# Splitting the query and key tiles of the latent attention two heads ahead and taking its scores in three passes: a case on one core of Trainium2

## The reference, cut to what matters

```python
q = (_rms_norm(cq, q_norm) @ w_uq).reshape(b, s, H, MLA_NOPE + MLA_ROPE)       # 64 + 32 per head
...
kv = (_rms_norm(ckv, kv_norm) @ w_ukv).reshape(b, s, H, MLA_NOPE + MLA_V)
k_nope, v = kv[..., :MLA_NOPE], kv[..., MLA_NOPE:]
...
sc = (jnp.einsum('bqhd,bkhd->bhqk', qn, k_nope) + jnp.einsum('bqhr,bkr->bhqk', qr, k_rope)) * scale
p, _ = _probs(sc, k_pos[None, :] <= t[:, None])
return jnp.einsum('bhqk,bkhd->bqhd', p.astype(v.dtype), v)
```

## Time and profile before

| | |
|---|---|
| median of three runs | 3776.79 us (3770.28 to 3781.73) |
| time of the profiled execution | 3777.02 us |
| its span | 3775.1 us |
| PE busy | 3430.8 us, 91% of the span |
| DVE busy | 2023.8 us, 54% |
| ACT busy | 1225.2 us, 32% |
| granted TensorE clock, mean | 0.927 of full |

### The profile page before, as it was taken

The page is one execution under the profiler, slowest core; times in us unless marked ns, Lnnn a source line. Parts: engine busy times, 40 slices in busy tenths (PEclk is TensorE's granted clock), DMA queues, the critical chain, the costliest instruction groups (busy, mean ns, idle before and its releaser), DMA issues.

```text
span 3775.1 us, 46102 instructions
## 1 busy us (share of the span) xinstructions
PE 3430.8 (91%) x16505; PEld 2822.2 (75%) x16505; DVE 2023.8 (54%) x2745; ACT 1225.2 (32%) x1897; POOL 239.9 (6%) x206
## 2 busy tenths in 40 slices
PE   8999998999999999989999994498899966879999
PEld 6888776887888788865778882398688854867887
DVE  7753433647743675355465435676555356545553
ACT  3222321543222322233432222454333231533332
POOL 1000101001000100022010004300000011010000
PEclk9999995999989999988999996699899978999999
DMA  5532241014532353211045320265233221013332
GB/s 168 175 106 89 82 110 24 1 43 135 161 95 95 114 175 106 89 55 34 29 123 168 110 95 22 62 175 169 67 100 100 89 72 39 1 45 89 91 104 72
DMA packets 390900, 347.51 MB, mean 92 GB/s; under 512 B 11344, under 2 KB 343437, under 8 KB 390669
## 3 DMA queue, kind: packets, MB, share of 16 engines
q1 hardware_dynamic: 390797, 346.16, 30.7%
HBM read 344.02 MB, written 2.10 MB: 92 GB/s over the span
## 4 chain that ended last, share of the span: by engine, by line
PE 81%; DVE 10%; ACT 3%; issue 2%; POOL 2%; SPq 1%; DMA 0%; ACTq 0%; DVEq 0%; POOLq 0%
PE ps L802 24%; PE ps L803 23%; PE ps L804 23%; PE ps L890 4%; PE ps L879 2%; PE ps L1285 2%; POOL sq_sum L2229 2%; ACT w_hi L1338 1%; DVE w_lo L1351 1%; DVE rstd L1716 1%; PE ps L867 1%; DVE a_lo L1693 1%; DVE x_T L2213 1%; PE ps L998 1%; DVE sq_att L2009 1%
## 5 line engine op out<-in xcount | busy, mean ns | idle before, releaser
L802 PE MATMUL ps<-a_hi,w_hi 128*128 128x512 f32 (+1 forms) x2968 | 1144.5, 386 | 134.8 <-DVE a_lo L1977 43.8
L803 PE MATMUL ps<-a_lo,w_hi 128*128 128x512 f32 (+1 forms) x2968 | 1129.9, 381 | 0.0
L804 PE MATMUL ps<-a_hi,w_lo 128*128 128x512 f32 (+1 forms) x2968 | 1128.9, 380 | 0.0
L802 PEld LDWEIGHTS ps<-a_hi,w_hi 128*128 128x128 f32 x2968 | 570.1, 192 | 279.3 <-issue 115.2
L1351 DVE TENSOR_TENSOR w_lo<-w_raw,w_hi 128x1024 fp32r<-128x1024 f32 (+1 forms) x536 | 636.3, 1215 | 183.4 <-ACT w_hi L1338 168.8
L1338 ACT ACTIVATE w_hi<-w_raw 128x1024 fp32r<-128x1024 f32 (+1 forms) x536 | 549.6, 1044 | 308.0 <-PE ps L804 306.1
L804 PEld LDWEIGHTS ps<-a_hi,w_lo 128*128 128x128 f32 x2968 | 571.1, 192 | 104.0
L803 PEld LDWEIGHTS ps<-a_lo,w_hi 128*128 128x128 f32 x2968 | 572.2, 193 | 100.9 <-issue 1.0
L802 PE MATMUL ps<-hs_hi,w_hi 128*128 128x512 f32 (+1 forms) x1232 | 465.1, 378 | 2.8 <-DVE w_lo L1351 1.5
L803 PE MATMUL ps<-hs_lo,w_hi 128*128 128x512 f32 (+1 forms) x1232 | 464.0, 377 | 0.0
L804 PE MATMUL ps<-hs_hi,w_lo 128*128 128x512 f32 (+1 forms) x1232 | 463.5, 376 | 0.0
(11 more groups left out here) (281 smaller groups left out, 3240.5 us busy)
## 6 DMA issues: line engine op xcount, KB each, us to landing
w_raw<-in_ffn_w_up SPq DMA_DIRECT2D x220, 512.0 KB, 4.9
w_raw<-in_ffn_w_down SPq DMA_DIRECT2D x154, 512.0 KB, 3.4
ada_raw<-in_ada_w SPq DMA_DIRECT2D x96, 512.0 KB, 3.8
w_raw<-in_ffn_w_gate SPq DMA_DIRECT2D x88, 512.0 KB, 5.0
w_raw<-in_ev_w_in SPq DMA_DIRECT2D x20, 512.0 KB, 3.7
w_raw<-in_attn_w_qkv SPq DMA_DIRECT2D x16, 512.0 KB, 4.8
w_raw<-in_ev_w_out SPq DMA_DIRECT2D x8, 512.0 KB, 4.0
w_raw<-in_mla_w_out SPq DMA_DIRECT2D x8, 512.0 KB, 3.4
```

The lines of the kernel that those rows point to most:

```text
L802: mm(dst, hi, rhi, start=start, stop=False)
L803: mm(dst, hi, rlo, start=False, stop=False)
L804: return mm(dst, lo, rhi, start=False, stop=stop)
```

## The change

The latent attention now passes two tiles for each query and each key, so that `three` takes its scores. The hi parts lie in a small ring `qk_mla_hi` of two heads; the lo parts are written over `q_mla` and `k_mla` (`q_mla_lo` and `k_mla_lo` are the same memory under the type fp32r). The four splits of heads 0 and 1 are made ahead of the attention, ACT waiting until all rotary parts and all keys are there. Those of head u+2 are made at the end of unit u, two in each of the units 0 to 13. A tile of gains moves out of the memory that the ring takes.

```diff
+        mla_gain = sb("mla_gain", [P, 2], F32)
...
-        mla_gain = arena("mla_gain", [P, 2], F32, 89984)
+        q_mla_lo = arena("q_mla_lo", [P, 16, SEQ], F32R, 0)
+        k_mla_lo = arena("k_mla_lo", [P, 16, SEQ], F32R, 32768)
+        qk_mla_hi = arena("qk_mla_hi", [P, 2, 2, SEQ], F32R, 81920)
...
-            heads = [dict(q=(q_mla[0:96, h, :],), k=(k_mla[0:96, h, :],), v=lambda kb, h=h: v_mla[:, kb, h * HD:h * HD + HD],
-                          out=o_mla[:, :, h * HD:h * HD + HD], gate=None, need=None) for h in range(16)]
-            ph.att = attention_plan(heads, "causal", work=work_mla, mask=mask_mla[:, :], dim=HD)
+            ph.qk0 = qk_hi_s.plan(32)
+            qk_lo_s.plan(32)
+            heads, splits = [], []
+            for h in range(16):
+                splits.append([(q_mla[0:96, h, :], qk_mla_hi[0:96, h % 2, 0, :], q_mla_lo[0:96, h, :]),
+                               (k_mla[0:96, h, :], qk_mla_hi[0:96, h % 2, 1, :], k_mla_lo[0:96, h, :])])
+                heads.append(dict(q=splits[h][0][1:], k=splits[h][1][1:], v=lambda kb, h=h: v_mla[:, kb, h * HD:h * HD + HD],
+                                  out=o_mla[:, :, h * HD:h * HD + HD], gate=None, need=ph.qk0 + 2 * h + 2))
+            ph.first_splits = splits[0] + splits[1]
+            ph.att = attention_plan(heads, "causal", work=work_mla, mask=mask_mla[:, :], dim=HD, later=splits[2:])
...
+                    act.wait_ge(rd_s.sem, ph.rd0 + 17)
+                    act.wait_ge(kc_s.sem, ph.kc0 + 1)
+                    act.wait_ge(ev_s.sem, ph.ev0 + 20)
+                    for split in ph.first_splits:
+                        qk_hi(split)
                     attention(ph.att)
...
-                    attention(ph.att)
+                    for n, split in enumerate(ph.first_splits):
+                        qk_lo(split, ph.qk0 + n)
+                    attention(ph.att, ph.qk0 + 4)
```

## The result

The changed kernel takes 3840.8 us (median of four runs, 3830.22 to 3865.88) against 3775.25 of the kernel before in the same measurement: a ratio of 1.0182, 95% interval 1.013 to 1.0234. It is slower by 1.8%, some 65 us; 3783.1 was forecast, and the range ended at 3793. (The ratios of this text are those on record with their intervals; the quotient of the two medians can differ from them in the third decimal.) A second execution beside one of the kernel before on the same chip gave 3831.69 against 3773.37, +58.3.

What follows compares the result with a forecast made beforehand. PE, busy for 91% of the span, was taken to bound the kernel. The start's 0.7 us and the split loop's 5.6 made +6.3 against 3777.0, itself 0.2 over the median: 3783.1 us, range over all cases 3775 to 3793.

Steps and rivals of the forecast that it cites:

- Those two slacks: In the latent attention: ACT idle 2.33 us ahead of its first take, DVE's take 1.82 us ahead of PE's value product.
- Term 2: Splits in the loop between DVE and ACT: 6.20 us a head instead of 5.80, +5.6 us over 14 units.
- Term 1: Latent attention, three score passes for one: a head 0.04 us longer as in `dil`, +0.6 us if nothing else changed.
- Term 3: Start of the attention: first splits delay PE 2.01 us, part won back; net +0.7 us, between 0 and 2.0.
- The 1.3 us that were to be won back at half clock: Start of the attention: three passes at 1.2 GHz save 1.2 us in head 0, some 0.1 in head 1.
- The table load: Start of the attention: loading the exponential's table, 1.28 us, is covered by head 0's scores; uncovered at most 1.28.
- The rival with the falling clock: Latent attention: PE's new short waits lower the granted clock, 6.72 us a head, 3790.6 us in all; chance 0.22.
- The loop does not bind: Latent attention: ACT and DVE overlap better, PE keeps 5.84 us a head, 3778.3 us in all; chance 0.10.
- The passes are worth more: Latent attention: passes run at the rate of wide ones, 0.6 us less a head, 3768.1 us in all; chance 0.04.

Runs made afterwards that it cites:

- splits_wait: Changed kernel with one fp32 score product and lo parts in tiles nothing reads, PE's wait for the splits kept: 3830.09 us, ratio 1.0126 to the kernel before.
- passes_alone: Changed kernel without splits inside the attention, all heads scored in three passes from the tiles of heads 0 and 1: 3777.06 us, ratio 0.9993 to the kernel before.
- splits_alone: Changed kernel with one fp32 score product, lo parts in tiles nothing reads, and no PE wait for splits: 3789.22 us, ratio 1.0014 to the kernel before.
- three_ahead: Changed kernel with splits one head earlier: heads 0 to 2 ahead, unit u splits head u + 3: 3790.85 us, ratio 1.0022 to the kernel before.
- filler: Changed kernel with eight added products on PE ahead of its wait for the splits, output unchanged: 3825.13 us, ratio 1.0137 to the kernel before.
- early_both: Changed kernel with splits moved within the unit: ACT's ahead of its take of chunk 1, DVE's of chunk 2: 3782.31 us, ratio 0.9985 to before.

## Why the prediction was wrong

**The step that failed is the first reading of who waits.** "Those two slacks are what the new splits have to fit into" counts two waiters, ACT's take and the value product that needs DVE's take. There is a third, PE's scores, which wait for `qk_lo_s` by the `need` that the change adds. Term 2 took `nsa` as the model; there the splits are for tiles that `dil` reads much later, so nobody on PE waited for them, and that is the difference that decides. The rows of before would have given the price: PE's scores begin at 1802.33, and ACT's last exponential for the next head ends with this row's 0.19:

```profile
1808.24 0.19 ACT L1401 ACTIVATION_READ_ACCUMULATOR scores_mla<-scores_mla,stats 128x1 f32 x1
```

That is 6.10 us from a head's scores to ACT being free, then 0.65, 0.61, 0.69 and 0.06 for the splits: 8.11 us a head. splits_wait measured 8.05 in its heads at full clock.

**Term 1** was mis-sized in a favourable direction: 5.56 us a head measured (passes_alone), 5.84 taken from `dil`, with 5.74 as its lower bound. `dil`, with its 64 rows, was not the price of this head. **Term 2** as worked out was right for what it described: 6.20 forecast, 6.18 measured (splits_alone, three_ahead). It was not the loop that bound. **Term 3**: the delay of 2.01 us was 2.1 in every kernel in which PE's first scores wait for the first splits as the change orders them. The 1.3 us that were to be won back at half clock did not come. The scores of head 0 take 3.66 us (1771.60 to 1775.26 in the changed kernel) where 3.2 was worked out from wide passes: a pass over 128 columns steps by 0.21 to 0.24 there, not by a quarter of 0.43. And the clock rose later. Before, the window of 4 us from 1766 has 0.70; in early_both the window as far behind its own first score product has 0.50:

```profile
1766.00:1770.00 4.00, 4.00 (x13) 2.43 (x12) 1.54 (x7) 1.19 (x4) 0.00 (x0) 0.70 0.00 0
1773.30:1777.30 4.00, 4.00 (x16) 3.60 (x15) 2.83 (x9) 2.02 (x6) 0.00 (x0) 0.50 0.00 0
```

PE is busy throughout both; why it rose later was not settled. To the scores of head 2 it is 12.24 us in early_both (1769.55 to 1781.79) and 11.22 before (1762.11 to 1773.33). So the start costs 2.1 + 1.0 = 3.1 us there, over the forecast's 0.7 and over its upper bound of 2.0. The table load was covered.

**The rival with the falling clock** had the cause and the size wrong. The clock fell to 0.73 and cost 25.9 us, but not through the short waits named there: in splits_alone and three_ahead PE waits 0.35 to 0.6 us in each head and the clock holds 1.00. With 2.0 us of idle a head it falls, and with the same time filled (filler) it does not. The Trainium skill (TensorE: Matmul & The Clock Gate, section A second HAM failure mode: psum-queue depth-cycling) tells of a kernel in which short idles between groups of matmuls make the clock go to and fro; the traces of the latent attention agree at 2.0 us a head and not at 0.6. `nsa` has 0.36 us of idle in the head of the earlier trace rows and stretches at 0.76 all the same, so the length of the wait does not decide alone, and what makes the clock fall in `nsa` stays open.

"The loop does not bind" was not the case in the changed kernel, whose loop was longer still; early_both shows that it holds for another order. "The passes are worth more" had 0.6 us a head; passes_alone has 0.24.

## What to carry to other kernels

When work is moved ahead of its use, count the distance at the first reader on every engine, not at the engine that looks like the user: here PE scores head u + 2 at the start of unit u + 1, so a split at the end of unit u comes at the last moment, and one at the start of unit u (early_both), or a whole head earlier (three_ahead), does not hold PE's scores up. Before a stage of the same program is taken as the model of a new one, check that the same waits end there. And a wait of TensorE in a loop is to be priced twice, once for its length and once for the clock: 29.0 and 25.9 us here, though waits of up to 0.6 us a head cost nothing by the clock.

## What the runs showed of the hardware that was not expected

A stretch of products and transposes can stay at the low clock with PE never idle. In the trace of splits_alone the first layer's `dil`, which no experiment touches, had five heads in a row at 9.98 to 10.18 us, where the kernel before has 5.84. A window within them:

```profile
800.00:830.00 30.00, 30.00 (x133) 27.18 (x132) 9.26 (x36) 9.50 (x32) 0.00 (x0) 0.53 0.00 1
```

PE is busy for all of the 30 us, at a granted clock of 0.53. The same stage in the kernel before:

```profile
750.00:795.00 45.00, 43.98 (x316) 37.41 (x316) 23.73 (x96) 23.60 (x76) 0.00 (x0) 1.00 0.01 1
```

The changed kernel's first trace has two such heads at the same place (10.11 and 9.36), its second none. From trace to trace the first layer's attention (from the first take of `nsa` to the last of `dil`) was 139.3 to 176.9 us long, a difference greater than most effects looked for here; that is why the lengths of the latent attention are compared above, which agree to 0.1 us between two traces of one kernel. What puts `dil` at one level or the other was not settled. `nsa` has 16 units (eight heads in two branches) and `dil` eight, and not eight each, so the window from 719 to 760 in the earlier trace rows is of units of `nsa` without a split. They too have three passes and no wait to speak of, and the argument on them stands; but `dil`, which held 1.00 in that trace, is the stage that stood at 0.53 in another execution.

With the same wait of 2.0 us a head, the clock was 0.88 with one fp32 product (splits_wait) and 0.73 with three fp32r passes (the change).

The steps between the scores and what stands beside them differ between `dil` and the latent attention. From the last score pass over 64 rows to the next transpose is 0.32 us and from the last value product to the next scores 1.04 in `dil`; over 96 rows it is 0.23 (1805.52 to 1805.75) and 0.92 (1808.39 to 1809.31). These two make 0.21 of the 0.28 us by which a head of passes_alone is shorter than one of `dil`. That the rows of the tile make the difference was not tested by itself. The two starts in `dil` that the earlier trace rows does not have, ahead of its 775.33 and of its 779.07:

```profile
775.01 0.39 PE L804 MATMUL ps<-F_more,F_r 64*128 64x512 f32 x1
...
778.03 1.10 PE L890 MATMUL ps<-v_tok,probs_T_even 128*128 128x64 f32 x8
```
